# Last layer norm divided among three engines, two output passes in quarters, and other places for three constant loads and a Silu table

## The chip, the cores and the metric

One core of a Trainium2 chip. The metric is the device time of one execution in microseconds (us), median over runs. The engines are TensorE (PE; PEld is its weight load), VectorE (DVE), ScalarE (ACT), GpSimd (POOL) and SyncE (SP), which issues most DMAs; ACT issues some as well. Each engine works through its own list of instructions in order and waits on semaphores.

## The reference, cut to what matters

256 tokens with 1024 features, in float32. `first_block` is two layers: a retention branch (four heads) and a latent-attention branch (MLA, 16 heads), each followed by a norm, a residual and a gated projection. `second_block` is one layer:

```python
proj = (layer_norm(x) * (1.0 + sc1) + sh1) @ w_in
merged = sigmoid(gate_a) * ya + sigmoid(gate_b) * yb      # ya: causal convolution branch, yb: pooled branch
x = layer_norm(ALPHA * x + g1 * (merged @ w_out), ln1_g, ln1_b)
h = layer_norm(x) * (1.0 + sc2) + sh2
v, gt = split(causal_dwconv(h @ w_up, w_dw_f, b_dw_f), 2)
x = layer_norm(ALPHA * x + g2 * ((gelu(gt) * v) @ w_down), ln2_g, ln2_b)
```

The last line, with 22 tiles of 128 hidden features into `w_down`, is the end of the kernel. A layer norm subtracts the mean, divides by the root of the variance, and multiplies and adds a row of gains and offsets.

## The kernel before, in words

**Weights.** All weights come from HBM in blocks of 128x1024 float32 (512 KB) through a ring of four slots (`raw`). To keep float32 accuracy each block is taken apart by `split`: ACT copies it to `whi` in fp32r (L991), DVE subtracts to get `wlo` (L1522), and PE adds three products, hi x hi, lo x hi and hi x lo. SP issues the load of a block once `lo_done` tells that the slot's former block has been split (L353, L354). ACT and DVE split three blocks ahead of PE (`AHEAD`). The name `B_...` numbers the blocks of a stage: `B_HEAD` retention heads (12 blocks each), `B_MIN` and `B_MG` the MLA input and gate strips, `B_GRP` the MLA groups, `B_WO` the output product of the mixer, `B_UP` and `B_DN` the feed-forward part.

**Products.** There are two forms. A strip (`products`, L489) has 128x128 weights stationary and 256 tokens moving. A row product (`row_products`, L562) has 128 tokens stationary and 512 output features moving. In the row form the two tiles of tokens (t = 0, 1) and the two halves of the output features (h = 0, 1) have four banks of PSUM: `half(2, t, h)`. `token_pass` makes one half for one tile of tokens, and tells `tok_done` behind tile 0 and `pe_done` behind tile 1.

**The start.** ACT issues five DMAs in a row (L1182 to L1186): `c_row`, the retention mask `maskd` (512 KB), `tri` (192 KB, the causal mask of the MLA groups), `cnt` (32 KB, counts of the pool branch) and `praw` (256 KB, features of the first gated projection). Behind them stand the splits of blocks B_HEAD+4 and B_HEAD+5 and the Sin for the rotary table. DVE waits for mask, tri and cnt together (L1763) before its first head. A loop runs heads 0 to 2; head 3 is written out.

**The MLA input.** ACT copies the transposed latents out of PSUM (`qkv_hi(0)`, `qkv_hi(1)`, L1043) with splits between them, then splits B_MG+1, then evacuates two gate strips with Silu (`gate_evac_one`, L1288). PE begins the first group's key product (L499 with S) only when the first of these has freed its bank (`act_free`, L783).

**First norm of the second block (B_WO).** DVE multiplies a half of the output by a row of gates (`gated_half`, L1650), adds the residual (L1660, or L2138), takes its statistics (`half_stats`, L1610), and after both halves the variance (L1614). ACT takes the root (L1020), DVE the reciprocal (L1571). Two norms follow one another, and PE waits for their result (L1625) before its next transposes (L610); 14 filler products (`hold`, L603) stand before them.

**The end (B_DN).** PE makes h = 0 for both tiles of tokens, then blocks 0 to 6 of h = 1 for both, then blocks 7 to 10 for tile 0, then for tile 1. DVE does everything of the last norm but the root:

```python
def last_norm(n, t):
    variance(t)
    inverse_of(n, t)
    for part, c0, c1 in OUT_PARTS:
        if part == t:
            c = slice(c0, c1)
            step(stt(X[:, t, c], X[:, t, c], mv[:, t, 0:1], ROW_C[:, c], ALU.subtract, ALU.mult))
            stt(X[:, t, c], X[:, t, c], rs[:, t, 0:1], ROW_D[:, c], ALU.mult, ALU.add).then_inc(final, 1)
```

`step` makes DVE wait for its own instruction. `OUT_PARTS` is ((0, 0, 1024), (1, 0, 768), (1, 768, 1024)): tile 0 in one piece, tile 1 in 768 and 256 columns. SP (`finish`, L341) waits for each part and issues its store. These two instructions are L2237 and L2238.

Of the kernel before, what the change touches and what calls it, by code (L numbers as in the profile page):

```python
# [24 lines left out]
ALU = mybir.AluOpType  # L25
AX_X = mybir.AxisListType.X
ACT = mybir.ActivationFunctionType

P = 128
# [105 lines left out]
def program(nc, x_in, pre_in, p_in, pos_in, cols_in, rows_in, mask_in, tri_in, cnt_in, ident_in, ada_in, c_row, g_rows, w, out):  # L135

    ctx = ExitStack()
    with ctx:
        def sb(name, shape, dt=F32):
            return ctx.enter_context(nc.sbuf_tensor(name, shape, dt))  # L140

        def sem(name):
            return ctx.enter_context(nc.semaphore(name))
# [42 lines left out]
        rs = sb("rs", [P, 2, 2])  # L186
        bst = sb("bst", [P, 2, 12])
        mv = sb("mv", [P, 2, 2])
# [91 lines left out]
        f_ready, fh_ready, fl_ready = sem("f_ready"), sem("fh_ready"), sem("fl_ready")  # L280
        stored = sem("stored")

        def col(name, t=0, n=1):
# [54 lines left out]

        OUT_PARTS = ((0, 0, D), (1, 0, 768), (1, 768, D))

        def finish(sp):  # L341

            for n, (t, c0, c1) in enumerate(OUT_PARTS):
                sp.wait_ge(final, n + 1)
                sp.dma_start(out[:, t, c0:c1], X[:, t, c0:c1]).then_inc(stored, 16)
            sp.wait_ge(stored, 16 * len(OUT_PARTS))
# [139 lines left out]
        def _(pe):  # L486
# [89 lines left out]
            def token_pass(base, t, h, a, j0, n, before=(), flip=0):  # L576
# [10 lines left out]
                if t == 0:  # L587
                    last.then_inc(tok_done, 1)

            def both_tokens(base, h, a, n, j1, before=(), flip=0, j0=0):  # L590
# [363 lines left out]
            both_tokens(B_WO, 0, H, 4, 4, [(merged_lo, j + 1) for j in range(4)])  # L954
            token_pass(B_WO, 0, 1, H, 0, 4)
            token_pass(B_WO, 1, 1, H, 0, 4)
# [12 lines left out]
            both_tokens(B_DN, 0, Y, 11, 11, [(fl_ready, j + 1) for j in range(11)])  # L969
            both_tokens(B_DN, 1, Y, 11, 7)  # L970
            token_pass(B_DN, 0, 1, Y, 7, 11)
            token_pass(B_DN, 1, 1, Y, 7, 11)


        @block.scalar
        def _(act):
# [206 lines left out]
            act.dma_start(maskd[:], mask_in).then_inc(in_const, 16)  # L1183
            act.dma_start(tri[:], tri_in).then_inc(in_const, 16)
            act.dma_start(cnt[:], cnt_in).then_inc(in_const, 16)
            act.dma_start(praw[:], p_in[0]).then_inc(in_p, 16)  # L1186
            split(B_HEAD + 1)
# [315 lines left out]
            for j in range(15, 19):  # L1503
                split(B_DN + j)
            var_root(7, 0)
            var_root(8, 1)


        @block.vector
        def _(dve):  # L1510
# [100 lines left out]

            def variance(t):

                nc.vector.bn_aggr(mv[:, t, :], bst[:, t, :]).then_inc(row_var, 1)  # L1614

# [146 lines left out]
            dve.wait_ge(trig_ready, 1)  # L1762
            dve.wait_ge(in_const, 16 * 3)  # L1763

# [124 lines left out]
            def group(o, i, gates):  # L1889
# [82 lines left out]
                tt(dyn(Yl, 4 * i + 4 * o, 4), YG, f32(dyn(Yh, 4 * i + 4 * o, 4)), ALU.subtract).then_inc(y_ready, 1)  # L1972

            with dve.Fori(0, 3) as i:
                group(0, i, 4)
# [165 lines left out]
            split(B_WO + 4)  # L2141
            half_stats(0, 0)
            residual(1, 0)

            def first_norm(n, t):

                variance(t)
                if t == 0:
# [75 lines left out]
            for j in range(13, 16):  # L2224
                split(B_DN + j)
            residual_half(1, 0, ROW_G2)
            for j in range(16, 19):
                split(B_DN + j)

            def last_norm(n, t):  # L2230

                variance(t)
                inverse_of(n, t)
                for part, c0, c1 in OUT_PARTS:
                    if part == t:
                        c = slice(c0, c1)
                        step(stt(X[:, t, c], X[:, t, c], mv[:, t, 0:1], ROW_C[:, c], ALU.subtract, ALU.mult))  # L2237
                        stt(X[:, t, c], X[:, t, c], rs[:, t, 0:1], ROW_D[:, c], ALU.mult, ALU.add).then_inc(final, 1)  # L2238

# [3 lines left out]
            dve.wait_ge(row_d, 16)  # L2243
            last_norm(11, 0)
            used(B_DN + 21)
            residual_half(1, 1, ROW_G2)
            last_norm(12, 1)


        @block.gpsimd  # L2250
        def _(pool):
# [77 lines left out]
            pool.wait_ge(pads, 1)  # L2329

            pool.wait_ge(act_free, A_WP + 2 + 2)
            for g, window in enumerate(WINDOWS):
# [8 lines left out]
                gtt(PO[:, g, :], src[:, 16:16 + T], U[:, g, 16:16 + T], ALU.subtract).then_inc(pooled, 1)  # L2341
                pool.wait_ge(pooled, g + 1)

def _features(a):
# [126 lines left out]
```

## Time and profile before

| | us |
|---|---|
| median of 3 runs | 822.09 (821.45 to 822.82) |
| the profiled execution | 821.67 |
| its span, first to last instruction | 819.6 |
| busy: PE, DVE, ACT, POOL | 803.2, 660.8, 457.1, 43.4 |
| idle of PE found in its waits, the first start left out | about 5 |
| granted clock of PE, mean | 0.996 |

A line of the timeline has start, duration, engine, line of the kernel and operation, out<-in, the shape, and in brackets how long the engine sat idle before it and what ended that. "x2" means that two neighbouring instructions were merged. ACTq and SPq are the queues' DMA issues.

### The profile page before, as it was taken

How to read it: one execution, taken by the hardware profiler on the slowest of the kernel's cores; microseconds unless marked ns; L12 is line 12 of the kernel's file. 1: busy time of each engine (PE TensorE's matmuls, PEld its weight loads, DVE VectorE, ACT ScalarE, POOL GpSimd, SP SyncE). 2: the span in 40 equal slices, each digit the busy share in tenths (PEclk: the TensorE clock that was granted, in tenths of full speed). 3: DMA queues.
4: the chain of work that ended last, by engine and by line, in shares of the span. 5: the costliest groups of instructions: out<-in, count | busy, mean ns of one | idle time of the engine just before them, and what ended most of it. 6: DMA issues, size and time to landing. Idle time of an engine off the chain costs nothing.

```text
span 819.6 us, 14985 instructions
## 1 busy us (share of the span) xinstructions
PE 803.2 (98%) x5394; PEld 729.8 (89%) x5394; DVE 660.8 (81%) x1043; ACT 457.1 (56%) x682; POOL 43.4 (5%) x58
## 2 busy tenths in 40 slices
PE   9999999999999999999999999999999999999995
PEld 9899999988778999999987889988988999999884
DVE  5979888786966887787967877999898898888466
ACT  6464545555646666657565536105853877777340
POOL 0009000000011000000000000060000000000000
PEclk9999999999999999999999999999999999999998
DMA  6957575679744757473749572445652566566541
GB/s 244 370 192 261 209 257 192 243 244 359 269 143 167 233 179 253 137 277 112 284 159 325 211 251 95 144 154 197 204 209 111 196 214 205 188 215 217 199 156 51
DMA packets 49002, 170.57 MB, mean 208 GB/s; under 512 B 6080, under 2 KB 6720, under 8 KB 48960
## 3 DMA queue, kind: packets, MB, share of 16 engines
q1 hardware_dynamic: 40896, 143.23, 50.0%
q10 hardware_dynamic: 8064, 26.78, 9.4%
q8 instruction: 26, 0.43, 0.2%
q14 instruction: 16, 0.13, 0.1%
HBM read 168.93 MB, written 1.06 MB: 207 GB/s over the span
## 4 chain that ended last, share of the span: by engine, by line
PE 74%; DVE 15%; ACT 4%; issue 4%; DMA 2%; DVEq 1%; ACTq 0%
PE bank L499 11%; PE bank L501 11%; PE bank L500 11%; PE bank L567 9%; PE bank L569 8%; PE bank L568 8%; DVE bank L2012 4%; DVE wlo L1522 3%; PE bank L513 2%; PE bank L704 2%; PE bank L705 2%; DMA ada_raw<-ada_in 2%; PE bank L706 2%; DVE ada_raw L1534 1%; PE bank L610 1%
## 5 line engine op out<-in xcount | busy, mean ns | idle before, releaser
L991 ACT ACTIVATE whi<-raw 128x1024 fp32r<-128x1024 f32 (+1 forms) x236 | 244.1, 1041 | 186.9 <-PE bank L501 76.0
L1522 DVE TENSOR_TENSOR wlo<-raw,whi 128x1024 fp32r<-128x1024 f32 (+1 forms) x236 | 283.0, 1212 | 60.2 <-ACT whi L991 58.2
L499 PE MATMUL bank<-H,whi 128*128 128x256 f32 x816 | 228.8, 280 | 0.6 <-DVE wlo L1522 0.4
L501 PE MATMUL bank<-H,wlo 128*128 128x256 f32 x816 | 225.7, 277 | 0.0
L500 PE MATMUL bank<-H,whi 128*128 128x256 f32 x816 | 225.6, 277 | 0.0
L499 PEld LDWEIGHTS bank<-H,whi 128*128 128x128 f32 x816 | 153.3, 188 | 2.3 <-issue 1.2
L500 PEld LDWEIGHTS bank<-H,whi 128*128 128x128 f32 x816 | 153.4, 188 | 0.1
L501 PEld LDWEIGHTS bank<-H,wlo 128*128 128x128 f32 x816 | 153.2, 188 | 0.0
L567 PE MATMUL bank<-whi,Y 128*128 128x512 f32 x216 | 84.7, 392 | 0.3 <-DVE wlo L1522 0.3
L569 PE MATMUL bank<-whi,Y 128*128 128x512 f32 x216 | 84.2, 390 | 0.0
L568 PE MATMUL bank<-wlo,Y 128*128 128x512 f32 x216 | 84.2, 390 | 0.0
L1534 DVE CUSTOM_DVE_ANT_0 ada_raw<-ada_raw,crow 128x1024 f32<-128x1024 f32 x48 | 60.5, 1260 | 10.0 <-DMA ada_raw<-ada_in 9.4
L499 PE MATMUL bank<-Y,whi 128*128 128x256 f32 x176 | 49.5, 281 | 0.8 <-ACT G L1149 0.8
L567 PEld LDWEIGHTS bank<-whi,Y 128*128 128x128 f32 x216 | 40.6, 188 | 9.2 <-DVE wlo L1522 0.9
L501 PE MATMUL bank<-Y,wlo 128*128 128x256 f32 x176 | 48.6, 276 | 0.0
L500 PE MATMUL bank<-Y,whi 128*128 128x256 f32 x176 | 48.6, 276 | 0.0
L569 PEld LDWEIGHTS bank<-whi,Y 128*128 128x128 f32 x216 | 40.5, 188 | 8.6
L568 PEld LDWEIGHTS bank<-wlo,Y 128*128 128x128 f32 x216 | 40.6, 188 | 8.3
L2012 DVE SCALAR_TENSOR_TENSOR bank<-WK,cols,bank 128x256 f32<-128x256 f32 x116 | 47.4, 483 | 0.4
L567 PE MATMUL bank<-whi,H 128*128 128x512 f32 x112 | 44.3, 395 | 0.4 <-DVE H L1593 0.3
L569 PE MATMUL bank<-whi,H 128*128 128x512 f32 x112 | 43.7, 390 | 0.0
L568 PE MATMUL bank<-wlo,H 128*128 128x512 f32 x112 | 43.6, 389 | 0.0
(265 smaller groups left out, 1312.7 us busy)
## 6 DMA issues: line engine op xcount, KB each, us to landing
ada_raw<-ada_in ACTq DMA_DIRECT2D x48, 512.0 KB, 5.4
raw<-w_head SPq DMA_DIRECT2D x47, 512.0 KB, 4.4
raw<-w_up SPq DMA_DIRECT2D x42, 512.0 KB, 3.3
raw<-w_down SPq DMA_DIRECT2D x22, 512.0 KB, 4.3
raw<-w_uq SPq DMA_DIRECT2D x24, 384.0 KB, 3.1
raw<-w_ret_out SPq DMA_DIRECT2D x16, 512.0 KB, 5.7
raw<-w_mla_gate SPq DMA_DIRECT2D x16, 512.0 KB, 4.5
raw<-w_mla_out SPq DMA_DIRECT2D x16, 512.0 KB, 5.2
```

The source lines that it names most:

```text
L499: mm(o, hi, a[:, 0, :], start=start, stop=False)
L500: mm(o, hi, a[:, 1, :], start=False, stop=False)
L501: last = mm(o, lo, a[:, 0, :], start=False, stop=stop)
L513: last = mm(o[:, tok(t)], raw[:, s, c], WT[:, t, c], start=(k == 0), stop=(k == 7))
L567: mm(o, a[:, k0 + k, 0, tok(t)], hi[:, c], start=start and k == 0, stop=False)
L568: mm(o, a[:, k0 + k, 0, tok(t)], lo[:, c], start=False, stop=False)
L569: last = mm(o, a[:, k0 + k, 1, tok(t)], hi[:, c], start=False, stop=stop and k == 1)
L704: mm(o, Hh[:, kk, tt], whi[:, s, c], start=(kk == 0), stop=False)
L991: activation(parts_of(b + (per * i if isinstance(i, int) else 0), n)[0], block_in(b, n), ACT.Copy).then_inc(hi_done, 1)
L1522: tt(lo, block_in(b, n), f32(hi), ALU.subtract).then_inc(lo_done, 1)
L1534: nc.vector.tensor_tensor_reduce(ada_raw[:, n, :], ada_raw[:, n, :], crow[:], 1.0, 0.0, ALU.mult, ALU.add, macc[:, a:a + 1]).then_inc(ada_ ...
L2012: stt(total[:, c, :], x, w_tap, CT[:, c, :], ALU.mult, ALU.add).then_inc(conv_tap[c], 1)
```

## The change

It has four parts.

1. The last norm is divided. Behind the reciprocal DVE also makes `centre` = -mean x rs. For tile 0 DVE does columns 0 to 255; for tile 1, columns 0 to 767. The other columns go to ACT (`scale`: Identity with scale rs and bias centre) and then to POOL (`weighted`: times ROW_C, plus ROW_D). SP waits for tile 1's POOL part before DVE's.
2. The last half of B_WO for tile 0, and h = 1 of B_DN for tile 1, are made in two quarters of 256 features, the first in the old bank, the second in `GD[0]`. DVE multiplies, adds and takes statistics by quarters. The statistics of h = 0 are by quarters too there, so that the variance is made of four parts.
3. The loads of tri, cnt and praw move from the start to between the loop over heads 0 to 2 and head 3. DVE waits for tri and cnt only before the MLA groups; POOL waits before its branch.
4. The Silu table is loaded between `split(B_MG)` and `qkv_hi(1)`, and the first gate strip is evacuated before `split(B_MG + 1)`.

```diff
+        bst = sb("bst", [P, 2, 24])
+        centre = sb("centre", [P, 2])
...
-        OUT_PARTS = ((0, 0, D), (1, 0, 768), (1, 768, D))
+        LEFT, LEFT_1 = slice(0, 256), slice(0, 768)
+        RIGHT, RIGHT_1 = slice(256, D), slice(768, D)
+        OUT_PARTS = ((0, 0, 256, final, 1), (0, 256, D, pool_final, 1), (1, 768, D, pool_final, 2), (1, 0, 768, final, 2))
...
+            def quarter(t, q):
+                return half(2, t, 1)[:, 0:T] if q == 0 else GD[0][:, 0:T]
+
+            def quarter_products(base, j, t, q, a, n):
+                hi, lo = parts_of(base + n + j)
+                for k in range(2):
+                    o, kk, c = quarter(t, q), 2 * j + k, slice(512 * k + T * q, 512 * k + T * q + T)
+                    mm(o, a[:, kk, 0, tok(t)], hi[:, c], start=kk == 0, stop=False)
+                    mm(o, a[:, kk, 0, tok(t)], lo[:, c], start=False, stop=False)
+                    last = mm(o, a[:, kk, 1, tok(t)], hi[:, c], start=False, stop=kk == 2 * n - 1)
+                return last
...
-            token_pass(B_WO, 0, 1, H, 0, 4)
+            quarter_pass(B_WO, 0, H, 0, 4)
...
-            both_tokens(B_DN, 1, Y, 11, 7)
+            for j in range(7):
+                loaded(B_DN + 11 + j)
+                row_products(B_DN + 11 + j, half(2, 0, 1), 0, Y, 2 * j, j == 0, False)
+                quarter_products(B_DN, j, 1, 0, Y, 11)
+                quarter_products(B_DN, j, 1, 1, Y, 11).then_inc(pe_done, 1)
             token_pass(B_DN, 0, 1, Y, 7, 11)
-            token_pass(B_DN, 1, 1, Y, 7, 11)
+            quarter_pass(B_DN, 1, Y, 7, 11)
...
             act.dma_start(maskd[:], mask_in).then_inc(in_const, 16)
-            act.dma_start(tri[:], tri_in).then_inc(in_const, 16)
-            act.dma_start(cnt[:], cnt_in).then_inc(in_const, 16)
-            act.dma_start(praw[:], p_in[0]).then_inc(in_p, 16)
...
             with act.Fori(0, RET_HEADS - 1) as i:
                 head(i, True)
+            act.dma_start(tri[:], tri_in).then_inc(in_const, 16)
+            act.dma_start(cnt[:], cnt_in).then_inc(in_const, 16)
+            act.dma_start(praw[:], p_in[0]).then_inc(in_p, 16)
             head(RET_HEADS - 1, False)
...
             split(B_MG)
+            table(ACT.Silu)
             qkv_hi(1)
...
+            gate_evac_one(B_MG, 0, 0)
             split(B_MG + 1)
-            gate_evac_one(B_MG, 0, 0)
             gate_evac_one(B_MG + 1, 1, 1)
...
+            def scale(t, c):
+                act.wait_ge(centre_ready, t + 1)
+                activation(X[:, t, c], X[:, t, c], ACT.Identity, bias=centre[:, t:t + 1], scale=rs[:, t, 0:1]).then_inc(scaled, 1)
+
             var_root(7, 0)
+            scale(0, RIGHT)
             var_root(8, 1)
+            scale(1, RIGHT_1)
...
             residual(0, 0)
             split(B_WO + 4)
-            half_stats(0, 0)
+            quarter_stats(0, 0)
+            quarter_stats(0, 1)
+            dve.wait_ge(quarter_done, 1)
+            residual_quarter(0, 2, ROW_G1)
             residual(1, 0)
...
-            residual_half(0, 1, ROW_G1)
+            residual_quarter(0, 3, ROW_G1)
...
             dve.wait_ge(tok_done, K_DN + 1)
             residual_half(0, 1, ROW_G2)
...
-            last_norm(11, 0)
+            variance(0)
+            last_norm(11, 0, LEFT)
+            dve.wait_ge(quarter_done, 2)
+            residual_quarter(1, 2, ROW_G2)
             used(B_DN + 21)
-            residual_half(1, 1, ROW_G2)
-            last_norm(12, 1)
+            residual_quarter(1, 3, ROW_G2)
+            variance(1, 4)
+            last_norm(12, 1, LEFT_1)
...
+            def weighted(n, t, c):
+                pool.wait_ge(scaled, t + 1)
+                gtt(X[:, t, c], X[:, t, c], ROW_C[:, c], ALU.mult).then_inc(pool_out, 1)
+                pool.wait_ge(pool_out, n)
+                gtt(X[:, t, c], X[:, t, c], ROW_D[:, c], ALU.add).then_inc(pool_final, 1)
```

## Rows read from the trace of the kernel before

**Rows 1.** The page: span, and busy time by engine

```profile
span 819.6 us, 14985 instructions
PE 803.2 (98%) x5394; PEld 729.8 (89%) x5394; DVE 660.8 (81%) x1043; ACT 457.1 (56%) x682; POOL 43.4 (5%) x58
```

**Rows 2.** Timeline at the start, ACT's queue, DVE and PE

```profile
17.14 0.45 ACTq L1184 DMA_DIRECT2D tri<-tri_in  x1
...
18.10 0.61 ACTq L1186 DMA_DIRECT2D praw<-p_in  x1
...
19.97 1.23 DVE L1522 TENSOR_TENSOR wlo<-ada_raw,whi 128x1024 fp32r<-128x1024 f32 x1 [1.48 <-ACT whi L991]
...
28.57 0.50 PE L704 MATMUL bank<-whi,H 128*128 128x512 f32 x1 [0.32 <-DVE wlo L1522]
```

**Rows 3.** Timeline at the MLA input, ACT and PE

```profile
264.86 1.07 ACT L991 ACTIVATE whi<-raw 128x1024 fp32r<-128x1024 f32 x1
267.49 0.38 ACT L1043 ACTIVATE S<-bank 128x256 fp32r<-128x256 f32 x1 [1.56 <-PE bank L610]
...
269.61 1.28 ACT L1288 ACT_TABLE_LOAD   x1
...
271.41 0.38 PE L499 MATMUL bank<-S,whi 128*128 128x256 f32 x1 [0.79 <-ACT G L1288]
```

**Rows 4.** Chain of waits: start, step, engine; 256 and 512 columns moving

```profile
262.00 0.11 PE bank L499
...
770.12 0.23 PE bank L569
```

**Rows 5.** Timeline of the first norm (B_WO), DVE and PE

```profile
615.75 0.69 DVE L1650 TENSOR_TENSOR Z<-bank,maskd 128x512 f32<-128x512 f32 x1 [0.77 <-PE bank L569]
...
624.63 1.11 PE L610 MATMUL bank<-ident,Z 128*128 128x128 f32 x8 [0.42 <-DVE Z L1625]
```

**Rows 6.** Timeline: a sum of 256 columns on DVE

```profile
26.75 0.42 DVE L1553 TENSOR_TENSOR WK<-WK 128x256 f32<-128x256 f32 x1
```

**Rows 7.** Timeline of DVE in the last norm

```profile
807.92 0.21 DVE L1614 BATCH_NORM_AGGREGATE mv<-bst 128x2 f32<-128x12 f32 x1
808.49 0.16 DVE L1571 RECIPROCAL rs<-rts 128x1 f32<-128x1 f32 x1 [0.36 <-ACT rts L1020]
...
811.21 0.68 DVE L1650 TENSOR_TENSOR Z<-bank,TAB 128x512 f32<-128x512 f32 x1
...
814.15 1.02 DVE L2237 SCALAR_TENSOR_TENSOR X<-X,mv,G 128x768 f32<-128x768 f32 x1
...
816.65 0.48 DVE L2238 SCALAR_TENSOR_TENSOR X<-X,rs,G 128x256 f32<-128x256 f32 x1
```

**Rows 8.** DMA issues in the last 15 us: size, us to landing

```profile
out<-X SPq DMA_DIRECT2D x1, 384.0 KB, 2.6
out<-X SPq DMA_DIRECT2D x1, 128.0 KB, 2.0
```

**Rows 9.** Timeline of POOL and DVE at work side by side, and POOL alone

```profile
60.02 2.74 POOL L2308 TENSOR_SCALAR G<-G,cols 128x256 f32<-128x256 f32 x2 [59.20 <-DVE Y L1815]
...
61.45 0.68 DVE L1549 TENSOR_TENSOR WK<-bank,TAB 128x512 f32<-128x512 f32 x1
...
74.71 1.29 POOL L2315 TENSOR_TENSOR G<-G 128x512 f32<-128x512 f32 x1
...
74.75 2.33 DVE L1522 TENSOR_TENSOR wlo<-raw,whi 128x1024 fp32r<-128x1024 f32 x1
...
533.05 0.64 POOL L2337 TENSOR_TENSOR WK<-WK 128x271 f32<-128x271 f32 x1 [27.40 <-ACT WK L1149]
```

**Rows 10.** Groups of ACT: the copy of 768 columns

```profile
L991 ACT ACTIVATE whi<-raw 128x768 fp32r<-128x768 f32 x20 | 16.9, 846 | 12.6 <-PE bank L501 8.9 <-PE bank L795 3.7
```

**Rows 11.** Timeline of ACT and DVE in retention head 3

```profile
139.56 1.06 ACT L991 ACTIVATE whi<-raw 128x1024 fp32r<-128x1024 f32 x1 [2.53 <-DMA raw<-w_head]
...
143.97 2.35 DVE L1522 TENSOR_TENSOR wlo<-raw,whi 128x1024 fp32r<-128x1024 f32 x2
```

More of the change, by code:

```diff
@@ L186, in program @@
         rs = sb("rs", [P, 2, 2])
-        bst = sb("bst", [P, 2, 12])
+        bst = sb("bst", [P, 2, 24])
+        centre = sb("centre", [P, 2])
         mv = sb("mv", [P, 2, 2])
@@ L281, in program @@
         stored = sem("stored")
+        quarter_done, centre_ready, scaled, pool_out, pool_final = (sem("quarter_done"), sem("centre_ready"), sem("scaled"),
+                                                                    sem("pool_out"), sem("pool_final"))
         def col(name, t=0, n=1):
@@ L336, in program @@
         block = ctx.enter_context(nc.Block())
-        OUT_PARTS = ((0, 0, D), (1, 0, 768), (1, 768, D))
+        LEFT, LEFT_1 = slice(0, 256), slice(0, 768)
+        RIGHT, RIGHT_1 = slice(256, D), slice(768, D)
+        OUT_PARTS = ((0, 0, 256, final, 1), (0, 256, D, pool_final, 1), (1, 768, D, pool_final, 2), (1, 0, 768, final, 2))
         def finish(sp):
-            for n, (t, c0, c1) in enumerate(OUT_PARTS):
-                sp.wait_ge(final, n + 1)
+            for t, c0, c1, done, n in OUT_PARTS:
+                sp.wait_ge(done, n)
                 sp.dma_start(out[:, t, c0:c1], X[:, t, c0:c1]).then_inc(stored, 16)
@@ L588, in token_pass, with quarter_pass @@
                     last.then_inc(tok_done, 1)
+            def quarter(t, q):
[8 more added lines that the diff above has]
+                return last
+            def quarter_pass(base, t, a, j0, n):
+                for q in range(2):
+                    for j in range(j0, n):
+                        if t == 0 and q == 0:
+                            loaded(base + n + j)
+                        last = quarter_products(base, j, t, q, a, n)
+                        if t == 1 and q == 1:
+                            last.then_inc(pe_done, 1)
+                    if q == 0:
+                        last.then_inc(quarter_done, 1)
+                    elif t == 0:
+                        last.then_inc(tok_done, 1)
             def both_tokens(base, h, a, n, j1, before=(), flip=0, j0=0):
@@ L1610, in half_stats, with quarter_stats, residual_quarter, variance @@
                 step(nc.vector.bn_stats(bst[:, t, 6 * h:6 * h + 6], X[:, t, 512 * h:512 * h + 512]))
-            def variance(t):
-                nc.vector.bn_aggr(mv[:, t, :], bst[:, t, :]).then_inc(row_var, 1)
+            def quarter_stats(t, q):
+                step(nc.vector.bn_stats(bst[:, t, 6 * q:6 * q + 6], X[:, t, T * q:T * q + T]))
+            def residual_quarter(t, q, row):
+                c = slice(T * q, T * q + T)
+                src = PB[2 + t][:, 512:512 + T] if q == 2 else GD[0][:, 0:T]
+                step(tt(WT[:, t, c], src, row[:, c], ALU.mult))
+                step(stt(X[:, t, c], X[:, t, c], ALPHA, WT[:, t, c], ALU.mult, ALU.add))
+                quarter_stats(t, q)
+            def variance(t, n=2):
+                nc.vector.bn_aggr(mv[:, t, :], bst[:, t, 0:6 * n]).then_inc(row_var, 1)
             def centred_rows(n, t, on_act=False):
@@ L1762, in _ @@
             dve.wait_ge(trig_ready, 1)
-            dve.wait_ge(in_const, 16 * 3)
+            dve.wait_ge(in_const, 16)
             def head(i, more):
@@ L1972, in group @@
                 tt(dyn(Yl, 4 * i + 4 * o, 4), YG, f32(dyn(Yh, 4 * i + 4 * o, 4)), ALU.subtract).then_inc(y_ready, 1)
+            dve.wait_ge(in_const, 16 * 3)
             with dve.Fori(0, 3) as i:
@@ L2141, in _ @@
             split(B_WO + 4)
-            half_stats(0, 0)
+            quarter_stats(0, 0)
+            quarter_stats(0, 1)
+            dve.wait_ge(quarter_done, 1)
+            residual_quarter(0, 2, ROW_G1)
             residual(1, 0)
             def first_norm(n, t):
-                variance(t)
+                variance(t, 4 - 2 * t)
                 if t == 0:
@@ L2225, in _, with last_norm @@
                 split(B_DN + j)
-            residual_half(1, 0, ROW_G2)
+            gated_half(1, 0, ROW_G2)
+            step(stt(X[:, 1, 0:512], X[:, 1, 0:512], ALPHA, WT[:, 1, 0:512], ALU.mult, ALU.add))
+            quarter_stats(1, 0)
+            quarter_stats(1, 1)
             for j in range(16, 19):
                 split(B_DN + j)
-            def last_norm(n, t):
-                variance(t)
+            def last_norm(n, t, c):
                 inverse_of(n, t)
[L2234 to L2238, printed above, removed]
+                stt(centre[:, t:t + 1], mv[:, t, 0:1], -1.0, rs[:, t, 0:1], ALU.mult, ALU.mult).then_inc(centre_ready, 1)
+                step(stt(X[:, t, c], X[:, t, c], mv[:, t, 0:1], ROW_C[:, c], ALU.subtract, ALU.mult))
+                stt(X[:, t, c], X[:, t, c], rs[:, t, 0:1], ROW_D[:, c], ALU.mult, ALU.add).then_inc(final, 1)
             dve.wait_ge(tok_done, K_DN + 1)
@@ L2329, in _ @@
             pool.wait_ge(pads, 1)
+            pool.wait_ge(in_const, 16 * 3)
             pool.wait_ge(act_free, A_WP + 2 + 2)
@@ L2342, in _ @@
                 pool.wait_ge(pooled, g + 1)
+            def weighted(n, t, c):
[3 more added lines that the diff above has]
+                gtt(X[:, t, c], X[:, t, c], ROW_D[:, c], ALU.add).then_inc(pool_final, 1)
+            pool.wait_ge(row_c, 32)
+            pool.wait_ge(row_d, 16)
+            weighted(1, 0, RIGHT)
+            weighted(2, 1, RIGHT_1)
 def _features(a):
```

## The prediction

> **What bounds the kernel now.** I read the page first: PE is busy for 803.2 of the 819.6 us [rows 1]. So a change saves time only where PE stands still, or behind its last product. There are few such places, and the timeline shows which of them the diff touches: a stall near 28 us, where DVE's split is late [rows 2]; one near 271 us, where PE waits for the Silu evacuation [rows 3]; one near 624 us, where it waits for the first norm [rows 5]; and the tail, in which DVE works alone from 811.21 [rows 7] to the last store. Everything else in the diff lies beside PE's products.
>
> **The start.** ACT's issues of tri, cnt and praw run from 17.14 to 18.71 (18.10 + 0.61), and DVE's split at 19.97 had idled 1.48 us for ACT [rows 2]. With the three gone, ACT's split, DVE's split, the rotary angles behind it and the next splits all come some 1.5 us earlier; and 480 KB less stand among the weights that they read. PE gains only what it lost: 0.32 us before the product at 28.57 [rows 2]. The product after a stall takes 0.50 instead of 0.39, and two lesser hesitations at the neighbouring block borders belong to the same lateness. Bounds: 0.3 and 0.8 us. I take 0.7, as a lead of 1.5 us covers all of them: -0.7.
>
> **The moved loads.** Each issue counts where it goes now: 1.6 us of ACT's queue between heads 2 and 3, and 480 KB ahead of the two ada loads. The first split behind them comes about 1 us later. What covers it is the lead of the splits: ACT already waits 2.53 us there for a weight block, until 139.56, and DVE splits that block (behind other work) at 143.97 [rows 11], 3.3 us after ACT is done with it. Cost 0. Without this cover it would be up to 1.6 us. The waits of DVE and POOL for tri and cnt now stand in later stages, long behind the landing: 0.
>
> **The Silu table.** After split(B_MG), which ends at 265.93, ACT idles 1.56 us until 267.49 for PE's transposes [rows 3]. The table load (1.28) and its one-column activation (0.2) fit into that, and end at about 267.4. Then ACT does its three copies out of PSUM and the first gate strip, whose products are long done. That strip's bank is free at about 269, while PE finishes its last gate strip at 270.6. So PE's wait of 0.79 us [rows 3] goes, with a little of the restart behind it. The split of B_MG+1 comes 0.4 us later; PE needs its block only behind the group's first 24 products of 0.11 and 12 of 0.23 us, 5.4 us on, so nothing is late next. Bounds 0.8 and 1.0: -0.9.
>
> **Quarters on PE.** A product with 512 columns moving steps by 0.23 us and one with 256 by 0.11 [rows 4], each with its own weight load. Two for one cost nothing: 0. The first quarter of a pass (24 products) is done 2.7 us before the second.
>
> **Quarters in B_WO.** On DVE a dependent instruction of 512 columns costs its 0.69 and 0.03 to the next, 0.72. Of 256 columns a sum takes 0.42 [rows 6] and a scalar-tensor-tensor 0.48 [rows 7]. No row has statistics of 256 columns; between 0.42 (the nearest shorter instruction) and 0.69 I take 0.45, as for 512 columns they cost just what a sum costs. With the gaps, three instructions make 1.45. Before tile 0's second half DVE now has two short statistics in place of a long one (+0.24) and the first quarter (+1.45), so 1.69 more, where it had idled 0.77 [rows 5]. So it begins the last quarter 0.92 late, and saves 2.17 - 1.45 = 0.72 in it. Net 0.2 late, and PE's wait of 0.42 [rows 5] grows by that: +0.2 (bounds -0.2 and +0.5; the 14 fillers in front allow no gain above 0.4). Saving on the half that comes last has here been paid in advance by an engine with no time to spare.
>
> **The tail without a conflict.** DVE's stretch for tile 1 starts when PE ends, 811.21 [rows 7], and DVE is just ready then. Quarter in place of half: 2.17 to 1.45, -0.7. The third instruction `centre` in front: +0.1. Columns 768 to 1023, two instructions of 0.5: -1.0. DVE would be done at 815.6, not 817.1. But the store behind it is now that of 768 columns, 2.6 us to landing instead of 2.0 [rows 8], and it is issued behind POOL's, 0.4 later. That leaves -0.7.
>
> **The conflict.** POOL and DVE work side by side on SBUF in the tail for the first time. The rows of the only earlier stretch show what that does: POOL's sum starts at 74.71 and takes 1.29; DVE's split, with two inputs in SBUF, starts at 74.75 and takes 2.33 instead of the 1.23 of [rows 2], which is POOL's end (76.0) and its own time behind it [rows 9]. A DVE instruction with one input in PSUM, at 61.45, takes its normal 0.68 beside POOL's 2.74 [rows 9]. So I reckon with exclusion, instruction by instruction, between POOL's two operations and DVE's `X*ALPHA + WT` and `X, ROW` operations, in the order in which they were issued. It is what decides this case. The Trainium skill, SBUF: State Buffer, section "Who interferes with whom", says so as a rule: a DVE instruction with two SBUF inputs contends with a GpSimd one that reads SBUF, and the other blocks for the whole instruction. The trace agrees, with 2.33 against 1.23.
>
> POOL's price: 0.64 for 271 columns and 1.29 for 512 [rows 9], the latter with a short wait for DVE's former instruction perhaps in it. In proportion that gives 1.81 and 1.94 for 768 columns; as a part of each is fixed, I take 1.75, and 0.62 for 256. ACT's scaling of 768 columns costs 0.85 [rows 10]. Tile 0: reciprocal at 808.49 [rows 7], centre until 808.9, DVE's two of 256 until 809.8, ACT until 809.75. POOL multiplies 809.8 to 811.55. DVE's product with PSUM ends at 810.15, its scalar-tensor-tensor must wait until 811.55 and ends at 812.0; POOL's addition was waiting and runs 812.0 to 813.75. DVE's statistics (0.45) and next product with PSUM pass freely until 812.85; its scalar-tensor-tensor waits until 813.75 and ends at 814.15, statistics until 814.65. Here DVE is 2.0 us behind the conflict-free course. Variance, root and reciprocal until 815.4 (0.77, as from 807.92 to 808.69, the end of the reciprocal and 0.04), centre, then 768 columns 815.55 to 816.55; POOL's multiplication of 256 (0.62) waits for that and ends at 817.2; DVE's second waits for POOL and ends at 818.15; POOL's addition waits for it and ends at 818.8. SP takes POOL's part first: issues at 818.8 and 819.2, the last lands at 821.8, and the 0.4 that stands now between the last landing (817.15 + 2.0) and the end of the span makes 822.2. Tail: 822.2 - 819.6 = **+2.6**.
>
> **Sum.** -0.7 - 0.9 + 0.2 + 2.6 = +1.2, a span of 820.8. The profiled execution took 821.67 with its span of 819.6; the median of the runs is 0.42 above that, and I put the change on it: 822.09 + 1.2 = 823.3. A measurement of this kernel can tell about 0.2%, 1.6 us, from no change; the forecast lies inside.
>
> **Rivals.**
> (a) *No conflict for these instructions.* Rows 9 show it for a subtraction on DVE, not for a scalar-tensor-tensor. If it passes, the tail gives -0.7 and the whole -1.4 + -0.7 = -2.1: 820.0. For: POOL's share of the work is then really free. Against: both are instructions with two tensors from SBUF. A half-way case, in which DVE loses a few tenths each time, ends near 821.5. Chance of the two 0.22.
> (b) *The moved loads collide* (slower). Place: head 3's beginning. DVE works in order, and its first ada sum there waits for a load that now stands behind 480 KB and 1.6 us of issues. ACT's wait of 2.53 [rows 11] shows that the DMA is busy there. It decides once DVE's split at 143.97 is more than 1 us late, the lead that it has over PE; each further tenth goes into the time, up to 1.6 us of issue and 1.2 us of transfer less that 1 us, so +1.8 at most, with +1.2 a fair middle: 824.5. Against: the 3.3 us between ACT's split and DVE's use of the same block, and a queue that at this place moves only three extra loads. Chance 0.1.
> (c) *The quarters are bound by the weight loads.* PEld's 729.8 us for 5394 loads [rows 1] are 0.135 us each at least; if that and not the step of 0.11 held with tokens stationary, the 180 products of 256 columns would cost 0.025 more each, +4.5: 827.8. Against: the strips show 0.11 with a fresh weight load every time [rows 4]. Chance 0.02.
>
> Forecast: 0.66. Its own range is 822.4 to 824.6 (POOL's 768 columns between 1.6 and 1.95 us, the statistics, the start between 0.3 and 0.8). With (a) and (b) taken in, 819.9 to 824.7.
> Faster by over 0.2%: most of (a)'s clean form, 0.15, and what I may have missed at PE's stalls: 0.2. Slower by over 0.2%: the upper part of the forecast (0.18), (b), (c): 0.28. Within: 0.52.
>
> **What would show it.** At the start: no idle before PE's product near 28 us, DVE's split near 18.5. At 271: no wait of PE for the first Silu evacuation, and a table load at 266. In B_WO: PE's wait before L610 at 0.5 to 0.7, DVE's idle of 0.77 gone. In the tail: DVE's scalar-tensor-tensors of 256 columns with 1.2 to 2 us in place of 0.48 beside POOL's; POOL's last addition behind DVE's last instruction, at 7.5 us or more after PE's end. If they take 0.5 and the last DVE instruction ends 4.5 us after PE, (a) is right and the forecast wrong. If PE shows a new wait near 145, (b) is.

## The result and the profile after

The changed kernel takes 824.00 us, the median of ten runs (823.45 to 825.55), beside 822.20 us for ten runs of the kernel before on the same chip: a ratio of 1.002 [1.0011, 1.0028]. So it is slower, by 1.8 us, and the interval straddles the bound of 0.2%. The forecast was 823.3 (+1.2). The profiled execution took 823.45 with a span of 821.6, 2.0 us more than the span before; both profiled executions are faster than their kernel's median, by 0.5 us each. The head of the page:

```profile
span 821.6 us, 15185 instructions
PE 803.8 (98%) x5484; PEld 734.8 (89%) x5484; DVE 662.3 (81%) x1051; ACT 458.9 (56%) x685; POOL 49.2 (6%) x62
```

PE is again the bound for all but the tail. What the change did is best read as a **lead**: how much earlier than before a fixed landmark is reached. At the first K·Q product it is 0.6 us (33.5, before 34.1). DVE's split stands where the forecast put it, 1.3 us earlier than in [rows 2]:

```profile
18.67 1.23 DVE L1567 TENSOR_TENSOR wlo<-ada_raw,whi 128x1024 fp32r<-128x1024 f32 x1
```

At the key product of the first group it is 1.65 us (269.76, before 271.41 in [rows 3]), and the product waits for nothing. ACT's timeline, in which the table load now stands, then PE's:

```profile
265.25 1.28 ACT L1045 ACT_TABLE_LOAD   x1
266.79 0.38 ACT L1080 ACTIVATE S<-bank 128x256 fp32r<-128x256 f32 x1
267.81 0.40 ACT L1326 ACTIVATE G<-bank 128x256 f32<-128x256 f32 x1
```
```profile
269.76 0.28 PE L504 MATMUL bank<-S,whi 128*128 128x256 f32 x1
```

In B_WO the lead shrinks. PE's timeline there: the last product of the third block's first quarter, then a new wait, and further on the filler products and the transposes:

```profile
610.35 0.28 PE L606 MATMUL bank<-whi,H 128*128 128x256 f32 x1
611.25 0.39 PE L604 MATMUL bank<-whi,H 128*128 128x256 f32 x1 [0.62 <-DVE wlo L1567]
...
620.41 3.29 PE L636 MATMUL bank<-ones 128*128 128x128 f32 x28
623.54 1.04 PE L643 MATMUL bank<-ident,Z 128*128 128x128 f32 x8
```

The wait is for the fourth block's low part, which DVE splits from 609.97 to 611.20. Behind it the fillers L636 run straight into the transposes L643: the wait of [rows 5], 0.42 us for the norm, is gone. The lead is 1.73 us when DVE begins its residual behind the passes, 0.51 at the first filler (620.41, before 620.92) and 1.09 at the transposes (623.54, before 624.63). At the end of tile 0 it is 0.45: DVE starts there at 805.29, before at 805.74.

From there to the end of the span, a stretch that is called the tail from here on, went 13.8 us before and go 16.3 now. Its rows in the timeline (start, duration, engine, line, tile, idle before and its releaser):

```profile
805.29 0.69 DVE L1707 TENSOR_TENSOR Z<-bank,TAB 128x512 f32<-128x512 f32 x1 [3.09 <-PE bank L574]
808.44 1.03 ACT L1546 ACTIVATE X<-X,centre,rs 128x768 f32<-128x768 f32 x1 [0.43 <-DVE centre L2297]
809.64 1.83 POOL L2413 TENSOR_TENSOR X<-X,G 128x768 f32<-128x768 f32 x1 [262.81 <-ACT X L1546]
809.69 2.06 DVE L1666 SCALAR_TENSOR_TENSOR X<-X,Z 128x256 f32<-128x256 f32 x1
810.73 0.28 PE L606 MATMUL bank<-whi,Y 128*128 128x256 f32 x1
811.55 1.87 POOL L2415 TENSOR_TENSOR X<-X,G 128x768 f32<-128x768 f32 x1
812.25 0.42 DVE L1665 TENSOR_TENSOR Z<-bank,TAB 128x256 f32<-128x256 f32 x1
812.70 0.99 DVE L1666 SCALAR_TENSOR_TENSOR X<-X,Z 128x256 f32<-128x256 f32 x1
815.09 1.01 DVE L2298 SCALAR_TENSOR_TENSOR X<-X,mv,G 128x768 f32<-128x768 f32 x1
815.88 0.80 POOL L2413 TENSOR_TENSOR X<-X,G 128x256 f32<-128x256 f32 x1 [2.47 <-ACT X L1546]
816.13 1.36 DVE L2299 SCALAR_TENSOR_TENSOR X<-X,rs,G 128x768 f32<-128x768 f32 x1
816.76 1.32 POOL L2415 TENSOR_TENSOR X<-X,G 128x256 f32<-128x256 f32 x1
```

The reader is to see the 256-column instructions at 809.69 and 812.70: 2.06 and 0.99 us for work that takes 0.42. Each ends just behind POOL's instruction beside it (811.47 and 813.42), while the product with an input in PSUM at 812.25 takes its 0.42 under POOL's addition. PE's last product starts at 810.73, with a last step of 0.12; DVE is ready for its last quarter only at 812.25.

### The profile page after: what moved, and what is told of

It is laid out like the page before. It is cut to its first block, busy times and chain, and to the rows that moved or that the text cites. A ratio compares the mean times of both kernels' runs of the same rounds, so it can differ in the third digit from the quotient of the medians.

```text
span 821.6 us, 15185 instructions
## 1 busy us (share of the span) xinstructions
PE 803.8 (98%) x5484; PEld 734.8 (89%) x5484; DVE 662.3 (81%) x1051; ACT 458.9 (56%) x685; POOL 49.2 (6%) x62
## 4 chain that ended last, share of the span: by engine, by line
PE 72%; DVE 17%; issue 4%; ACT 3%; DMA 3%; DVEq 1%; POOLq 0%; POOL 0%; ACTq 0%; SPq 0%
PE bank L504 11%; PE bank L506 10%; PE bank L505 10%; PE bank L572 8%; PE bank L573 7%; PE bank L574 7%; DVE wlo L1567 5%; DVE bank L2070 4%; PE bank L518 3%; PE bank L738 2%; PE bank L737 2%; PE bank L739 2%; DVE ada_raw L1579 2%; DMA ada_raw<-ada_in 2%; PE bank L643 1%
## 5 line engine op out<-in xcount | busy, mean ns | idle before, releaser
L572 PE MATMUL bank<-whi,Y 128*128 128x512 f32 x194 | 76.3, 393 | 0.3 <-DVE wlo L1567 0.3
L573 PE MATMUL bank<-wlo,Y 128*128 128x512 f32 x194 | 75.7, 390 | 0.0
L574 PE MATMUL bank<-whi,Y 128*128 128x512 f32 x194 | 75.6, 390 | 0.0
L572 PEld LDWEIGHTS bank<-whi,Y 128*128 128x128 f32 x194 | 36.5, 188 | 8.1 <-DVE wlo L1567 0.7
L574 PEld LDWEIGHTS bank<-whi,Y 128*128 128x128 f32 x194 | 36.4, 188 | 7.7
L573 PEld LDWEIGHTS bank<-wlo,Y 128*128 128x128 f32 x194 | 36.5, 188 | 7.2
L2257 DVE SCALAR_TENSOR_TENSOR WK<-WK,cols 128x256 f32<-128x256 f32 x88 | 36.8, 480 | 6.0 <-ACT WK L1515 6.0
L572 PE MATMUL bank<-whi,H 128*128 128x512 f32 x104 | 41.2, 396 | 0.4 <-DVE H L1638 0.3
L573 PE MATMUL bank<-wlo,H 128*128 128x512 f32 x104 | 40.6, 390 | 0.0
```

Of the source, the lines that this page charges most:

```text
L572: mm(o, a[:, k0 + k, 0, tok(t)], hi[:, c], start=start and k == 0, stop=False)
L573: mm(o, a[:, k0 + k, 0, tok(t)], lo[:, c], start=False, stop=False)
L574: last = mm(o, a[:, k0 + k, 1, tok(t)], hi[:, c], start=False, stop=stop and k == 1)
L2257: stt(CV[:, c, :], UPAD[:, c, k:k + T], dcol("dwf", 4 * i + 4 * o + c + 44 * k), CV[:, c, :], ALU.mult, ALU.add).then_inc(cv_step, 1)
```

## The experiments

Theory: DVE's instructions with two SBUF inputs and POOL's exclude each other, and this costs about 3 us of tail that the parts at the start and at the Silu table only partly pay for. Rivals: the quarters themselves cost the time, on PE or on DVE; the moved loads cost something; the later store does. Times below are medians, but for e5_offsets, e6_silu and e7_loads, which ran once each; ratios are to the kernel before on the same chip. Where a span or a place is given it is one profiled execution; the same kernel's spans differ by up to 2 us between executions (821.5 to 823.5 for the changed one), so single places prove a term only where a row shows the wait itself.

**e1_moves: the kernel before, with the moved loads and the Silu table alone.**

```diff
-            act.dma_start(tri[:], tri_in).then_inc(in_const, 16)
-            act.dma_start(cnt[:], cnt_in).then_inc(in_const, 16)
-            act.dma_start(praw[:], p_in[0]).then_inc(in_p, 16)
...
                 head(i, True)
+            act.dma_start(tri[:], tri_in).then_inc(in_const, 16)
+            act.dma_start(cnt[:], cnt_in).then_inc(in_const, 16)
+            act.dma_start(praw[:], p_in[0]).then_inc(in_p, 16)
...
             split(B_MG)
+            table(ACT.Silu)
```

> The kernel before with only the moved loads and the moved Silu table. Theory: both leads are kept to the end, since nothing between head 3 and the end waits for a fixed time. PE's key product of the first MLA group starts at 269.8 instead of 271.4, DVE's last norm 1.6 us earlier than before, span 818.0, ratio to before 0.998. Rival (the lead is lost on the way, at head 3's loads or in DMA-bound stretches): the lead at 271 is there but not at the end, span 819 to 819.6, ratio 1.000.

Measured 820.63 us (820.15 to 820.93), ratio 0.9979 [0.997, 0.9988], span 818.5. It beats both kernels. PE's waits for the split near 28 us and for the Silu evacuation are gone, and the wait for the first norm stands as before (PE's waits: us in total, times, longest; then DVE's timeline, where it takes up tile 0's last half):

```profile
PE bank L610 <- DVE Z L1626: 0.4, 1, 0.4
```
```profile
804.70 0.69 DVE L1651 TENSOR_TENSOR Z<-bank,TAB 128x512 f32<-128x512 f32 x1 [3.06 <-PE bank L569]
```

From 804.70 to the end go 13.8 us, as before. So by the medians these two parts are worth 1.7 us (822.36 less 820.63), and everything else in the change costs 824.00 - 820.63 = 3.4 us. The trace shows less, and something of the rival. The lead is 2.0 us between 272 and 292 us, 1.5 at 295 and 1.05 at PE's last product. Most of the loss stands in the first MLA group: DVE waits there for a weight block, and PE, now early, waits for DVE (DVE's timeline, then PE's):

```profile
289.71 1.23 DVE L1535 CUSTOM_DVE_ANT_0 ada_raw<-ada_raw,crow 128x1024 f32<-128x1024 f32 x1 [0.40 <-DMA ada_raw<-ada_in]
```
```profile
292.81 0.71 PE L829 MATMUL bank<-WK 128*128 128x128 f32 x4 [0.27 <-DVE WK L1902]
```

The changed kernel keeps its lead at this place (1.80 and 1.73 us), so this loss differs between executions. How much of the lead a usual execution keeps is told by the medians alone.

**e2_norm_on_dve: the changed kernel with the last norm on DVE alone and its stores as before.**

```diff
-        OUT_PARTS = ((0, 0, 256, final, 1), (0, 256, D, pool_final, 1), (1, 768, D, pool_final, 2), (1, 0, 768, final, 2))
+        OUT_PARTS = ((0, 0, D, final, 1), (1, 0, 768, final, 2), (1, 768, D, final, 3))
...
-            weighted(1, 0, RIGHT)
-            weighted(2, 1, RIGHT_1)
```

> The changed kernel with the last norm back on DVE alone and the stores as before; quarters and moves stay. Theory (port conflict with POOL costs the tail): DVE's sums with two inputs in SBUF take 0.43 each instead of 2.06 and 0.99; from tile 0's last product to the end of the span some 14.7 us instead of 16.3, span 820.0, ratio 1.000 to before. Rival (the tail is long for another reason, as the quarters or the order of stores): these instructions stay above 1 us, span 821 or more.

Measured 822.86 us (821.7 to 823.49), ratio 1.0003 [0.9994, 1.0012]: 1.1 us less than the changed kernel. DVE's timeline:

```profile
811.34 0.42 DVE L1663 TENSOR_TENSOR Z<-bank,TAB 128x256 f32<-128x256 f32 x1
811.80 0.42 DVE L1664 SCALAR_TENSOR_TENSOR X<-X,Z 128x256 f32<-128x256 f32 x1
813.18 0.42 DVE L1664 SCALAR_TENSOR_TENSOR X<-X,Z 128x256 f32<-128x256 f32 x1
```

Without POOL beside them the same two instructions take 0.42 us. But the tail is 14.5 us (805.87 to 820.3), longer than the 13.8 of before: the first quarter, done long ago on PE, is reached by DVE only at 811.34, when PE ends (its last product starts at 811.30), since DVE is busy with tile 0's norm until then. On an engine that is behind, two quarters are just a half with three more instructions.

**e3_halves: the changed kernel with halves in both places, the norm still divided.**

```diff
-            quarter_pass(B_WO, 0, H, 0, 4)
+            token_pass(B_WO, 0, 1, H, 0, 4)
...
-            for j in range(7):
...
-                quarter_products(B_DN, j, 1, 0, Y, 11)
-                quarter_products(B_DN, j, 1, 1, Y, 11).then_inc(pe_done, 1)
+            both_tokens(B_DN, 1, Y, 11, 7)
             token_pass(B_DN, 0, 1, Y, 7, 11)
-            quarter_pass(B_DN, 1, Y, 7, 11)
+            token_pass(B_DN, 1, 1, Y, 7, 11)
```

> The changed kernel with halves in place of quarters in both places; the divided norm and the moves stay. Theory (a product with 256 columns moving and tokens stationary steps by 0.120 us, against half of 0.227, so that 180 of them cost 1.2 us, and the first quarter of B_WO needs its fourth block early and waits 0.6 for it): no wait of PE in B_WO for wlo, tile 0's half of B_DN is done at 804.1 instead of 805.3; the tail keeps a conflict of POOL and DVE; span 819.8, ratio 1.000. Rival (quarters cost PE nothing, the loss after 272 us lies elsewhere): done at 805.3 as in the changed kernel, span 821.5 or more, since DVE's stretch behind PE grows by 0.7.

Measured 821.97 us (820.64 to 822.55), ratio 0.9997 [0.9988, 1.0006]: the quarters cost 824.00 - 821.97 = 2.0 us. The wait for the fourth block's low part is gone and the 0.4 for the norm is back. The tail is 14.9 us (803.72 to 818.6), 1.3 less than with quarters. The profiled execution is the fastest of its eleven: DVE takes up tile 0's last half at 803.72, 1.0 us before e1_moves does after the same work, so the spans (821.6 and 818.6) overstate what the quarters cost, and the medians are to be read. In the tail DVE comes first this time, and POOL waits (DVE's timeline, then POOL's):

```profile
809.88 0.69 DVE L1713 SCALAR_TENSOR_TENSOR X<-X,Z 128x512 f32<-128x512 f32 x1
...
813.22 1.36 DVE L2289 SCALAR_TENSOR_TENSOR X<-X,rs,G 128x768 f32<-128x768 f32 x1
```
```profile
808.06 1.83 POOL L2401 TENSOR_TENSOR X<-X,G 128x768 f32<-128x768 f32 x1 [261.70 <-ACT X L1542]
809.97 2.27 POOL L2403 TENSOR_TENSOR X<-X,G 128x768 f32<-128x768 f32 x1
```

POOL's 2.27 are 0.6 of waiting and its own 1.7. With halves POOL's multiplication finds DVE idle in front of PE's last product; the quarter is what brought DVE into POOL's 768 columns.

**e4_psum: the changed kernel with tile 1's output kept in PSUM, so that no DVE instruction of the tail's critical part has two inputs in SBUF.**

```diff
+                step(tt(o, o, ROW_G2[:, c], ALU.mult))
+                step(stt(o, X[:, 1, c], ALPHA, o, ALU.mult, ALU.add))
...
+                x = PB[3][:, c] if t == 1 else X[:, t, c]
+                step(stt(x, x, mv[:, t, 0:1], ROW_C[:, c], ALU.subtract, ALU.mult))
+                stt(X[:, t, c], x, rs[:, t, 0:1], ROW_D[:, c], ALU.mult, ALU.add).then_inc(final, 1)
```

> The changed kernel, but DVE keeps tile 1 in PSUM from the product to the first of the two last operations, so that none of its instructions behind tile 0 has two inputs in SBUF; POOL and ACT do just what they do in the changed kernel. Theory (exclusion only against two SBUF inputs): DVE's 2.06 and 0.99 become 0.43 to 0.48, its last two 1.0 each, POOL's last two 0.6 to 0.8; DVE ends 4.4 us behind PE's end instead of 6.5; span 819.0, ratio 0.999. Rival (any DVE work beside POOL is slowed, or PSUM operands cost what the conflict did): 1 us and more in one of them, span 820.5 or more.

Measured 821.33 us (821.11 to 822.31), ratio 0.9988 [0.9979, 0.9997]. Same number of instructions, same columns, other operand places, and 2.7 us less than the changed kernel. The timeline:

```profile
810.01 1.83 POOL L2430 TENSOR_TENSOR X<-X,G 128x768 f32<-128x768 f32 x1 [262.94 <-ACT X L1546]
810.07 0.43 DVE L2299 SCALAR_TENSOR_TENSOR bank<-X,bank 128x256 f32<-128x256 f32 x1
811.48 0.43 DVE L2298 TENSOR_TENSOR bank<-bank,TAB 128x256 f32<-128x256 f32 x1 [0.52 <-PE bank L606]
811.95 0.43 DVE L2299 SCALAR_TENSOR_TENSOR bank<-X,bank 128x256 f32<-128x256 f32 x1
814.83 1.02 DVE L2316 SCALAR_TENSOR_TENSOR X<-bank,rs,G 128x768 f32<-128x768 f32 x1
815.34 0.72 POOL L2432 TENSOR_TENSOR X<-X,G 128x256 f32<-128x256 f32 x1
```

Under POOL's 1.83 us the scalar-tensor-tensor of 256 columns takes 0.43, and the last one of 768 takes 1.02 for 1.36. DVE again waits for PE (0.52) instead of running behind it. One thing more differs from the changed kernel: ACT's scaling of tile 1 reads PSUM too and takes 0.56 for 0.60. The tail is 13.9 us, so the conflict is worth 16.3 - 13.9 = 2.4 us. It is also just the tail of before (13.8): even free of the conflict the division brings nothing in the tail. DVE ends at 815.85 and POOL at 816.06, against DVE's 817.13 before, some 1.1 us earlier; but the last store is now the one of 384 KB, 2.6 us to landing instead of 2.0 [rows 8], and it is issued 0.4 us behind POOL's, 1.0 us together (stores of this kernel: size, median to landing):

```profile
out<-X SPq DMA_DIRECT2D x2, 384.0 KB, 2.6
out<-X SPq DMA_DIRECT2D x2, 128.0 KB, 1.9
```

**e5_offsets: the changed kernel with B_DN's blocks at another place in their ring slots.** It tests whether the 0.12 us of a quarter product is due to where its operand lies.

```diff
-    return b < B_MIN + 8 or B_MO <= b < B_WA or B_WO <= b < B_UP or b >= B_DN + 5
+    return b < B_MIN + 8 or B_MO <= b < B_WA or B_WO <= b < B_UP
```

> The changed kernel with the blocks of the last product B_DN+5 and later laid 16 and 48 elements into their slots, as blocks for strips are, and not at 0. It asks why a product with 256 columns moving and tokens stationary steps by 0.120 us where a strip's steps by 0.113. Theory (each product with weights moving has a fixed cost, some 0.0136 us, whatever it moves): the step of the quarters stays at 0.120 or above, and that of 512 columns at 0.227 to 0.230, as in the first five blocks of B_DN, which lie so already. Rival (the place in the slot makes it): the quarters step by 0.113, and tile 0's half of B_DN is done 0.6 us earlier than in the changed kernel after the same start.

One run: 824.04 us (before 822.78), span 822.0. The step moves, but not to 0.113. PE's last 48 products are the two quarters of tile 1. From the first to the last of them are 47 steps, 805.10 to 810.73 in the changed kernel, with the blocks at place 0, and 805.56 to 811.09 here, with the blocks at places 16 and 48:

```profile
805.10 0.28 PE L604 MATMUL bank<-whi,Y 128*128 128x256 f32 x1
```
```profile
805.56 0.28 PE L604 MATMUL bank<-whi,Y 128*128 128x256 f32 x1
...
811.09 0.28 PE L606 MATMUL bank<-whi,Y 128*128 128x256 f32 x1
```

That is 0.120 us a step at place 0 and 0.118 at 16 and 48: less than the theory allows, and far from the rival's 0.113. With 512 columns the place counts the other way. The kernel before shows it in itself. Its block B_DN+1 lies at 16 and 48, and B_DN+7 at 0; the first product of each and the one 12 steps later:

```profile
753.69 0.39 PE L567 MATMUL bank<-whi,Y 128*128 128x512 f32 x1
...
756.45 0.39 PE L567 MATMUL bank<-whi,Y 128*128 128x512 f32 x1
```
```profile
770.18 0.39 PE L567 MATMUL bank<-whi,Y 128*128 128x512 f32 x1
...
772.90 0.39 PE L567 MATMUL bank<-whi,Y 128*128 128x512 f32 x1
```

They step by 0.230 and 0.227 us, and in e5_offsets the second of them goes up to 0.230 as well (769.37 to 772.13). So two quarters in place of a half cost 0.013 us at place 0 (0.240 for 0.227), where the changed kernel has them, and 0.005 at 16 and 48 (0.235 for 0.230). The place is a part of the cause. It is not the whole: in the changed kernel's timeline of PE, 102 strip products (H moving, weights stationary, places 16 and 48) step by 0.113 each, 12 quarter products (weights moving, tokens stationary) by 0.119; first of each stretch and first behind it:

```profile
699.79 0.28 PE L504 MATMUL bank<-H,whi 128*128 128x256 f32 x1
...
711.36 0.28 PE L504 MATMUL bank<-H,whi 128*128 128x256 f32 x1
...
798.20 0.28 PE L604 MATMUL bank<-whi,Y 128*128 128x256 f32 x1
...
799.63 0.40 PE L572 MATMUL bank<-whi,Y 128*128 128x512 f32 x1
```

What makes the rest of the difference no run here shows.

**e6_silu and e7_loads: the kernel before with only the Silu table, and with only the moved loads** (each the matching part of e1_moves' diff; the loads also move DVE's and POOL's waits for them).

> The kernel before with only the Silu table and the first gate evacuation moved. Theory: the wait of 0.8 us before the key product of the first MLA group goes; that product starts at 270.5 instead of 271.4, and the start of the kernel is as before (0.3 us of wait near 28 us). Rival (the table load delays the copies of the latents, and they become the new wait): a wait of PE on turn_lo, shown as DVE or ACT's H copies, of 0.3 us or more in its place.

> The kernel before with only the loads of tri, cnt and praw moved. Theory: PE's wait near 28 us goes and with it 0.7 to 0.9 us; DVE's split at 19.97 comes near 18.6; the wait of 0.8 at the first MLA group stays. Rival (the loads collide in head 3): PE or DVE waits for w_head or ada_in between 134 and 150 that the kernel before doesn't have, and the lead is smaller behind head 3 than before it.

One run each: 821.24 us (span 819.5) and 821.23 (span 819.3), beside 822.78. With the table alone the group's key product waits for nothing, and the wait near 28 us stays; with the loads alone the reverse. So the traces show the two waits to be independent. They do not size the parts: 1.5 us each by one run against a median can't be right beside the 1.7 of both together, and in the two traces the leads shrink at the place that e1_moves shows, from 0.78 to 0.12 us and from 0.67 to 0.30. PE's waits, first of e6_silu, then of e7_loads (the second row there is 0.3 in the kernel before), and last ACT's waits of e7_loads between 130 and 152 us:

```profile
PE bank L704 <- DVE wlo L1523: 0.5, 2, 0.3
```
```profile
PE bank L499 <- ACT G L1288: 0.8, 1, 0.8
...
PE bank L567 <- DVE wlo L1522: 0.5, 1, 0.5
```
```profile
ACT whi L991 <- DMA raw<-w_head: 5.6, 3, 2.7
```

The last row is what the moved loads can do where they went: 5.6 us in three waits instead of 2.5 in one [rows 11], and DVE waits 0.6 us for ACT. The changed kernel's own trace has a single wait of 2.6 us there, so the collision doesn't come in every execution. PE doesn't see it here: its first K·Q product is 0.6 us early (33.5), its last 0.7 (146.6 against 147.3).

**e8_free_tail: e1_moves, with only tile 1's last 256 columns on ACT and POOL, DVE's first operation of 768 columns written to PSUM, and three last stores** (512 and 256 columns from SP, POOL's from ACT's queue).

```diff
+            act.wait_ge(pool_final, 1)
+            act.dma_start(out[:, 1, 768:D], X[:, 1, 768:D]).then_inc(stored, 16)
...
+            step(stt(PB[3][:, 0:768], X[:, 1, 0:768], mv[:, 1, 0:1], ROW_C[:, 0:768], ALU.subtract, ALU.mult))
+            for c in (slice(0, 512), slice(512, 768)):
+                stt(X[:, 1, c], PB[3][:, c], rs[:, 1, 0:1], ROW_D[:, c], ALU.mult, ALU.add).then_inc(final, 1)
```

> A version meant to beat both: the kernel before with both moves, halves everywhere, tile 0 wholly on DVE, and of tile 1 only columns 768 to 1023 on ACT and POOL; DVE writes the first of its two last operations into PSUM, so that the second has one input in SBUF; POOL's part is stored from ACT's queue, and DVE's 768 columns in two stores of 512 and 256. Theory: from tile 0's last product to the end of the span 13.2 us instead of 13.9 (1.0 us of DVE saved, 0.2 for centre and the split, 0.1 for the waits); ratio to before 0.997. Rival (POOL's path of scaling, two operations and its own store is longer than DVE's): POOL's addition ends behind DVE's last, tail 13.9 or more, ratio 0.998.

Measured 821.26 us (820.28 to 822.14), ratio 0.9981 [0.9972, 0.999], no better than e1_moves. DVE and POOL are done at 816.05 and 816.27, some 5.9 us after PE's last product starts (810.39), where DVE was done 6.4 us after it before (817.13 and 810.76), and the tail is still 14.2 us. The stores of this kernel show why:

```profile
out<-X SPq DMA_DIRECT2D x1, 256.0 KB, 2.6
out<-X SPq DMA_DIRECT2D x1, 128.0 KB, 2.7
out<-X ACTq DMA_DIRECT2D x1, 128.0 KB, 2.9
```

In the kernel before, the 128 KB that are issued last land in 2.0 us [rows 8], these two stores in 2.7 and 2.9, with three stores issued close together. What the engines gained, the landing took back.

## Why the prediction came out right

The forecast of +1.2 us stands beside a measured +1.8, by the mechanism named, with two terms too small. The near agreement of the tail is in part luck, as two larger sizes in it are wrong and cancel.

**Start, Silu table, moved loads** (-0.7, -0.9, 0): right. Leads of 0.6 and 1.65 us in the trace; e6_silu and e7_loads show the two waits to go one without the other, and e1_moves gives the sum, 1.7 us by medians. Rival (b) was refuted for PE: e7_loads has the collision at head 3 for ACT (5.6 us of waits against 2.5), and the cover named, ACT's lead over DVE, takes up all but 0.6 us of it for DVE and all for PE. The changed kernel's own trace doesn't show it (one wait of 2.6).

**The conflict** (+2.6 for the tail): right, 16.27 - 13.83 = +2.44. It was foreseen that the first scalar-tensor-tensor would end 6.3 us into the tail (812.0 on the time scale of before) and statistics follow; they start 6.5 us into it (811.78). e2_norm_on_dve and e4_psum show the cause in two ways: taking POOL away, and taking DVE's second SBUF input away, both return 2.06 and 0.99 us to 0.42. This refutes rival (a). The Trainium skill, SBUF — State Buffer, section "Who interferes with whom", has it that one of the two blocks for the other's whole instruction. The trace agrees for POOL's 768 columns, and e4_psum agrees with its other half, that an input in PSUM is free of it (0.43 under POOL's 1.83). The total was closer than its parts. Against a tail without the conflict the forecast had +3.3 (2.6 and 0.7), and e4_psum shows +2.4; the tail without the conflict was to be 0.7 shorter than before, and e4_psum shows no gain. The terms from which that 0.7 was made (-0.7, +0.1, -1.0, +0.6, +0.4) make -0.6, and behind the rest stand that PE's last pass is longer in quarters (DVE begins its last stretch 5.8 us into the tail, and 5.5 before) and that POOL ends 0.2 us behind DVE. In the course itself ACT's scaling costs 1.03, not the 0.85 of the rounding of 768 columns, and DVE's last instruction, reckoned to wait for POOL's whole multiplication, took 1.36 for 1.02.

**The term that failed** is in *Quarters on PE*: "Two for one cost nothing: 0". The 0.11 was read off strips, in which the tokens move, and both durations had two digits. With weights moving, two products of 256 columns take 0.239 to 0.240 us in the changed kernel and one of 512 took 0.227; over 90 pairs, at 0.012 to 0.013 each, that is 1.1 us. By place: 24 pairs in B_WO 0.3, 42 in B_DN's first seven blocks 0.5, 24 in the last pass 0.3. In those seven blocks the halves of tile 0 that now stand between quarters step by 0.231 too (782.71 to 784.10, six steps), 0.2 us in all, so that the lead falls by 0.6 up to the end of tile 0, from 1.09 to 0.45. Rival (c) had the right direction and a far too high price (4.5 us); its floor of 0.135 us a load does not hold, as the quarters step by 0.120. The place in the slot is a part of the cause (e5_offsets); why tokens moving are cheaper stays open.

**Quarters in B_WO** (+0.2) was mis-sized too, +0.6 (lead 1.73 to 1.09, with the 0.3 of the 24 pairs in it), and for another reason than given. I followed DVE into the norm and did not look at PE's side: the first quarter runs through the four blocks in 24 x 0.12 = 2.9 us where a half took 5.5, and so asks for the fourth block's low part before DVE has split it, 0.62 us of wait. The wait for the norm, forecast to grow to 0.6, vanished, because PE itself comes to it later.

**Sum in the trace**: -1.73 (to DVE's residual in B_WO) + 0.64 (B_WO) + 0.64 (up to the end of tile 0) + 2.44 (tail) = +2.0, the difference of the spans. By medians: e1_moves -1.7, the divided norm with halves +1.3 (e3_halves less e1_moves), the quarters on top +2.0, +1.6 in all from the 822.36 that the kernel before took beside them; beside the changed kernel's own runs the difference was 1.8.

## What to carry to other kernels

Work handed to GpSimd cost the tail 2.4 us here where DVE instructions beside it had two inputs in SBUF; with one input there, DVE's instructions kept their own length (e4_psum). Check this for the instructions that the handover lets start earlier too, and keep an intermediate in PSUM where it can be. A transfer at the end has its own price by size, order and company, so engines that are done 1.1 us earlier may leave the end where it was. Before splitting an output for an earlier start, ask whether the consumer is free at that time, whether the producer now reaches its inputs sooner than they are ready, and what a product costs beside its columns with the same operand moving and its operand at the same place.

## What the runs showed of the hardware

- Who waits follows the order of issue: with quarters POOL was first and DVE waited 1.6 us (2.06 for 0.42); with halves DVE was first by 0.09 us, kept its 0.69, and POOL waited (2.27 for 1.83). The waiting instruction ends 0.27 us after POOL's recorded end, less than its own 0.42 (811.75 against 811.47). Some 0.15 us of the two thus overlap; whether POOL lets go of SBUF before its record ends, or DVE's first part needs no SBUF, the rows don't tell apart.
- ACT with scale and bias from SBUF columns takes 1.03 us for 768 columns, where the rounding copy takes 0.85 [rows 10]; for 256, 0.60. The Trainium skill, ScalarE: Activation LUTs, section "What ACT_TABLE_LOAD costs", gives 93 ns for each operand of one element a partition; two of them are the 0.18 us between the rows, so the trace agrees. The forecast had taken the row and left the two operands out.
- POOL alone takes 1.83 us for a two-tensor operation of 768 columns and 0.72 for 256: 0.17 us and 0.55 for each 256 columns. DVE takes 1.02 for 768.
- Three stores issued close together land later, 2.7 and 2.9 us for 128 KB (e8_free_tail), than a store of 128 KB in the other kernels, 1.9 to 2.0. That their number or their two queues make the difference was not tested apart.
- The place of the moving weights in their slot changes a product's step: for 256 columns 0.120 us at place 0 and 0.118 at 16 and 48 elements, for 512 columns 0.227 and 0.230.
